# Two unread matrix products taken out of the routing chain ahead of an expert loop

## The reference

```python
def moe_swiglu(x, router_w, wi, wo):
    logits = (x @ router_w).astype(jnp.float32)
    top_v, top_i = lax.top_k(logits, TOP_K)
    gates = jax.nn.softmax(top_v, axis=-1)
    dispatch = jnp.sum(jax.nn.one_hot(top_i, N_EXPERTS) * gates[..., None], axis=-2)
    y = jnp.zeros_like(x)
    for e in range(N_EXPERTS):
        y = y + dispatch[..., e:e + 1] * swiglu(x, wi[e], wo[e])
    return y
```

## Time and profile before

| what | value |
|---|---|
| median of 3 runs | 1481.14 us (1480.47 to 1481.25) |
| profiled execution, its own time | 1485.01 us |
| profiled execution, span from first to last instruction | 1483.4 us |
| mean granted TensorE clock over the span | 0.998 |
| HBM traffic over the span | 336 GB/s |
| one record of the gather, L2654 | 379 ns (median of 72) |

### The profile page before, as it was taken

The page is one execution under the profiler, slowest core; times in us unless marked ns, Lnnn a source line. Parts: engine busy times, 40 slices in busy tenths (PEclk is TensorE's granted clock), DMA queues, the critical chain, the costliest instruction groups (busy, mean ns, idle before and its releaser), DMA issues.

```text
span 1483.4 us, 33187 instructions
## 1 busy us (share of the span) xinstructions
PE 1462.5 (99%) x14586; PEld 1010.5 (68%) x14586; DVE 533.0 (36%) x883; ACT 378.9 (26%) x707; POOL 92.7 (6%) x167
## 2 busy tenths in 40 slices
PE   9999999999999999999999999999999999999997
PEld 8989988999999999445545545455455455455443
DVE  6768976667765684301101101111111011011113
ACT  6556664568744533200000000000000000000011
POOL 0011150101000000100000000000000000000010
PEclk9999999999999999999999999999999999999999
DMA  7778732678755768999999999999999999999992
GB/s 260 296 264 321 252 136 87 209 260 298 272 177 179 281 242 334 417 402 418 399 419 419 400 419 419 400 419 419 401 419 419 400 419 419 401 419 419 419 416 116
DMA packets 81383, 500.19 MB, mean 337 GB/s; under 512 B 9737, under 2 KB 10073, under 8 KB 57057
## 3 DMA queue, kind: packets, MB, share of 16 engines
q1 hardware_dynamic: 70000, 460.41, 78.1%
q0 software_dynamic: 11248, 37.73, 7.5%
HBM read 474.15 MB, written 23.96 MB: 336 GB/s over the span
## 4 chain that ended last, share of the span: by engine, by line
PE 88%; DMA 4%; DVE 4%; ACT 3%; issue 1%; SPq 0%; ACTq 0%; DVEq 0%
PE PP L2674 39%; PE PP L2009 22%; PE PP L2684 20%; DMA ring<-in_wi 4%; DVE dlo L421 2%; ACT dhi L415 2%; PE PP L2127 1%; PE PP L2111 1%; PE PP L2538 0%; PE PP L2103 0%; PE PP L2089 0%; DMA ring<-in_mkv 0%; DMA ring<-in_b_in 0%; PE PP L2283 0%; PE PP L2293 0%
## 5 line engine op out<-in xcount | busy, mean ns | idle before, releaser
L2674 PE MATMUL PP<-ring,gen 128*32 128x448 f32 x6144 | 585.0, 539 | 1.2 <-issue 0.6
L2674 PEld LDWEIGHTS PP<-ring,gen 128*32 128x32 f32 x6144 | 286.3, 110 | 294.0 <-issue 292.7
L2684 PE MATMUL PP<-ring,gen 128*32 128x512 f32 x2688 | 295.7, 592 | 0.1
L2684 PEld LDWEIGHTS PP<-ring,gen 128*32 128x32 f32 x2688 | 165.9, 110 | 124.5 <-issue 113.2
L1170 ACT ACTIVATE ubuf<-PP 128x448 f32<-128x448 f32 x48 | 22.6, 545 | 782.2 <-PE PP L2674 782.2
L2009 PE MATMUL PP<-uh,dhi 128*128 128x264 f32 x736 | 214.3, 291 | 4.4 <-DVE dlo L421 4.2
L1947 DVE TENSOR_TENSOR gen<-ubuf,PP 128x448 f32<-128x448 f32 x48 | 26.9, 617 | 516.7 <-PE PP L2674 516.7
L2009 PE MATMUL PP<-ul,dhi 128*128 128x264 f32 x736 | 208.8, 284 | 0.0
L2009 PE MATMUL PP<-uh,dlo 128*128 128x264 f32 x736 | 208.6, 283 | 0.0
L421 DVE TENSOR_TENSOR dlo<-ring,dhi 128x2048 fp32r<-128x2048 f32 (+2 forms) x77 | 161.5, 2097 | 82.8 <-ACT dhi L415 82.6
L415 ACT ACTIVATE dhi<-ring 128x2048 fp32r<-128x2048 f32 (+2 forms) x77 | 135.3, 1758 | 101.0 <-PE PP L2009 66.7
(11 more groups left out here) (496 smaller groups left out, 1430.0 us busy)
## 6 DMA issues: line engine op xcount, KB each, us to landing
ring<-in_w_up SPq DMA_DIRECT2D x256, 896.0 KB, 20.7
ring<-in_w_down SPq DMA_DIRECT2D x112, 1024.0 KB, 20.2
ring<-in_wi SPq DMA_DIRECT2D x22, 1024.0 KB, 7.1
ring<-in_a_in SPq DMA_DIRECT2D x18, 1024.0 KB, 7.4
ring<-in_wo SPq DMA_DIRECT2D x16, 704.0 KB, 4.1
slot_rows<-ring POOLq DMA_DIRECT2D x25, 384.0 KB, 5.7
ring<-in_mkv SPq DMA_DIRECT2D x8, 1024.0 KB, 5.2
ring<-in_kc SPq DMA_DIRECT2D x8, 1024.0 KB, 9.6
```

The source lines that it names most:

```text
L2674: mm = pe.matmul(bank((c // KD % 2) * SG + g)[SL * q:SL * (q + 1), 0:FQ], xs[:, at_:at_ + SL], w[:, q * FQ:(q + 1) * FQ], start=(k == 0), ...
L2684: return pe.matmul(out[SL * quarter:SL * (quarter + 1), :], hT[:, at_:at_ + SL], w[:, k * D + h * 512:k * D + (h + 1) * 512], start=(j == ...
```

## The change

The two calls of `unread` are taken out. The helper stays defined but is not called any more. The wait for chunk 0 ahead of it stays. All other instructions, their order and their waits stay.

```diff
--- before.py
+++ after.py
@@ -2635,7 +2635,6 @@
                 for _ in range(count):
                     pe.matmul(bank(7), up_of(0)[:, 0:P], up_of(0)[:, 0:512], start=True, stop=True)
 
-            unread(1)
             pe.wait_ge(s("rt_sub"), 1)
             for j in range(2):
                 n = 3 - j
```

## The result

The kernel without the two products takes 1482.68 us (median of 20 runs, 1479.64 to 1486.59) against 1480.43 us before (20 runs, 1477.67 to 1483.15). The forecast was +1.3 us.

A forecast was written before the change was run, and what follows sets the result against it. The prediction took TensorE to bound the kernel, so a delay at the expert loop's start reaches the end. Direct gains 0 + 0, gather +1.2 and routing products +0.1 gave +1.3 us on 1481.14: 1482.4 us, range 1480.5 to 1484.3.

The forecast's parts named there:

- Direct gain of both products: Ahead of the counts and the gather: VectorE, not the products, releases TensorE's next instruction, so taking them out gains 0 us.
- The low bound of -0.3 us: At the second product: the gather could come at most 0.33 us earlier if the product's end released it.
- The clock falls over the bare chain: Routing chain, 592 to 600 us: without the products TensorE is sparse and its granted clock falls to 0.50 in some windows.
- The price, +1.3 us: Gather and routing products: 3.4 us of half clock, middle case from 595, costs 1.2 us plus 0.1 us.
- 4.7 to 5.8 us that I had named as the sign: At the gather: its 72 records should spread over 4.7 to 5.8 us in place of 4.09.
- The routing products, +0.1 us: L2642 to L2645: their latency grows if the clock is low; 0.1 us, being done before the fall in the middle case.
- the longer fall: Rival, chance 0.12: clock low from about 593, whole gather at half; +3.0 to +5.0 us, typically +3.3 us, 1484.4 us.
- Passed on in full: Expert loop: what moves its start moves the end by the same amount; stages keep 71.82 and 35.64 us.
- The rule of the Trainium skill: At the routing chain: frequent small idle times between matmul groups make the clock swing between two levels; gives the +1.3 us.
- The clock stays whole: Rival, chance 0.24: no clock fall around the routing chain; 1481.1 us, or 1480.8 with the second product's low bound.
- A stall that moves: Rival, chance 0.04: 2.2 us lost in the first up stage could vanish with a shorter instruction stream; 1478.9 us.

The follow-up runs named there:

- kernel with 40 products of ones: Against the kernel before: 40 in place of 24 unread products of ones at its very start, both removed products kept; ratio 1.0022.
- 8-column kernel: Against the kernel before: both products stay in place with the same weight loads but stream 8 columns each in place of 512; ratio 1.0021.
- 256-column one: Against the kernel before: both products stay in place but stream 256 columns each in place of 512; ratio 1.0010.
- the one with two at the second place: Against the kernel before: both products stand ahead of the gather, none stands ahead of the counts; ratio 1.0013.

## Why the prediction was right, and where its sizes were off

**Direct gain of both products, 0 us: right.** The kernel with the first alone has the gather 0.08 us behind VectorE and the loop at 8.82 us; the kernel with the second alone has L1837 3.09 us behind L1818, as before. The low bound of -0.3 us did not come true; the chain view's 0.94 us on a product was a name for time that VectorE set. One small thing was missed: without a product ahead of them the counts start 0.15 us behind L1828 (591.85 against 591.52 + 0.18), where it was 0.05 us; the 3.09 us just named show that this alone doesn't reach the chain.

**The clock falls over the bare chain: right.** All three profiles without the products show it; the kernel before shows it in neither of its two, nor does the kernel with 40 products of ones, which keeps both. That it is the work of the two products that prevents it is shown by the 8-column kernel: same instructions, same weight loads, the same loss. The 256-column one lies between, within the scatter of both.

**The price, +1.3 us: too small; measured 2.2 us.** The step that was mis-sized is the length of the half clock on the gather. I took 3.4 us of it, beginning in the middle at 595, from the one fall in the trace. In all three profiles it is twice as long and begins earlier, 592.5 to 599.3 in the first, where it covers the gather up to 599.3 and leaves its last 24 of 72 records at full clock. The gather's 72 records spread over 6.36 us, past the 4.7 to 5.8 us that I had named as the sign. The rate was right: the gather's groups of four products start 0.42 us apart (595.04 and 595.46 in the timeline above), and before the change 18 groups took 3.7 us, 0.21 us each; a factor of 2.0. The term measured 2.26 us in place of 1.2, and 1.67 and 2.12 us in the other two profiles.

**The routing products, +0.1 us: too small.** I had them done before the fall. In the first profile L2643 and L2644 ran at half clock: their records have 342 and 412 ns in the mean (262 ns for the 8-column product before), and +0.35 us reached the chain. In the other two profiles it was +0.81 us, where the fall came ahead of all of them, and +0.44 us. So where the long fall begins moves the loss between these products and the gather; the sum stays between 2.5 and 2.6 us.

```profile
L2644 PE MATMUL PP<-small,consts 128*128 128x32 f32 x2 | 0.6, 412 | 0.0
L2643 PE MATMUL PP<-small,ones 8*128 8x8 f32 x2 | 0.5, 342 | 0.0
```

So the mechanism was the forecast's and the course was the rival's, the longer fall that I gave 0.12; its price was over-stated at 3.3 to 5.0 us, because the gather isn't all at half and the routing products don't double (590.54 to 592.64, 2.10 us against 1.27 us, where all of them ran at half). The time itself, 1482.4 us forecast and 1482.68 us measured, agrees better than the price does, since the kernel before came out at 1480.43 us and not at 1481.14. So it is luck in part that the time lies in the range: the course that came true was the one with the smaller chance, at a price below its own. The two comparisons give ratios of 1.0015 and 1.0018, 2.2 and 2.7 us, and their intervals hold the 2.6 us of the profiles.

**Passed on in full: right.** The loop starts 2.6 us later behind L1818 and the span of the undisturbed profile of before is 2.6 us shorter. The stages kept their length, 72.37 and 36.05 us in both kernels; the 71.82 and 35.64 us that I named are the longest pieces of a stage in the chain, not the whole of it. TensorE's waits in the loop answer to the earlier trace rows:

```profile
PE PP L2672 <- DVE gen L1860: 0.6, 1, 0.6
```

There are none but that for the transposes at its start.

**The rule of the Trainium skill** ("TensorE: Matmul & The Clock Gate", section "A second HAM failure mode: psum-queue depth-cycling") that small idle times between groups of matmuls, often enough, make the clock swing is borne out in part. In two profiles of the changed kernel the clock fell to 0.50 after one idle gap of 1.24 us among small products, in the third while TensorE stood in that gap. The gap of 1.16 us ahead of the gather came only within the half clock. The same chain with the gaps filled kept 1.00. The section speaks of repeated cycles; here one sparse stretch did it.

**The rivals.** "The clock stays whole" is refuted. "A stall that moves" is refuted in its cause: the stall was absent in the second profile of the same kernel. It was also smaller than the 2.2 us that I took: the usual first stage is 72.37 us and not 71.82, so 74.04 us are 1.7 us too long.

## What to carry to other kernels

A product that nobody reads can be work for the clock. Before taking one out, look at what TensorE does around it and what dense work follows: here two products of 1.1 us in idle time saved some 2.2 us of an execution, most of it on the gather behind them. Such products cost nothing only while another engine sets the chain: with two at one place they held TensorE too long, by 0.5 us ahead of the counts and by as much ahead of the gather. Of the two here the first did most; whether the second earns anything is not shown, since the kernel with the first alone (1.0007, 0.9998 to 1.0016) can't be told from the one before. The chain of waits may put time on a product that only fills a wait: compare its end with the other inputs of the next instruction in the timeline.

## What the runs showed that I had not expected

The half clock lasted 6.8 us in each of the three profiles of the changed kernel and 3.4 us in those of the 8-column, the 256-column, the second-alone kernel and the one with two at the second place. It looks as if a little work in the chain halves the fall. The mean clock speaks against that for the 8-column kernel, as said there, and for the others it rests on one profile of each. The clock also falls away from this chain, in kernels with and without the two products: near 12 us in the first profiles of both, near 231 us in the first of the changed kernel and in four of the experiments. A mean granted clock over the span counts these falls too, so it alone doesn't say where the half clock was. Without a product ahead the first count product started 0.10 us later behind its releaser, at full clock. And a kernel of 1480 us scatters by 5 us from execution to execution while its comparison with itself comes out at 0.9999.
